# PV in an encoder layer's attention: the exponentials as stationary operand, the attention rows turned in the output projection

## What is computed

```python
def one_block(qblk):
    s = jnp.einsum('bqhd,bkhd->bhqk', qblk, k, preferred_element_type=jnp.float32) * scale
    p = jax.nn.softmax(s, axis=-1).astype(v.dtype)
    return jnp.einsum('bhqk,bkhd->bqhd', p, v)
...
att = _attention(q, k, v)
mix = jnp.concatenate([a, att], axis=-1) @ w_out[i]
h = h + gm[:, None, :] * mix
```

## Time and profile before

| | |
|---|---|
| runs of the kernel, us | 2167.23, 2167.49, 2172.06; median 2167.49 |
| profiled execution: span, us | 2165.6 |
| its own time beside the span | the profile gives none; the median lies 1.9 above the span |
| TensorE matmul busy | 2039.0 us, 94% |
| VectorE busy | 1208.9 us, 56% |
| ScalarE busy | 531.2 us, 25% |
| GpSimd busy | 296.2 us, 14% |
| attention, first row of maxima to first matmul of the output projection | 981.5 to 1336.4 us |

### The profile page before, as it was taken

One profiled execution on the slowest core, in us unless ns is written; L12 is line 12 of the kernel. 1 busy time (PEld: TensorE's weight loads), 2 busy tenths in 40 slices (PEclk: granted clock), 3 DMA queues, 4 the chain that ended last, 5 costly groups with the idle time before them and its releaser, 6 DMA issues.

```text
span 2165.6 us, 22126 instructions
## 1 busy us (share of the span) xinstructions
PE 2039.0 (94%) x8778; PEld 1615.0 (75%) x8778; DVE 1208.9 (56%) x1465; ACT 531.2 (25%) x690; POOL 296.2 (14%) x218
## 2 busy tenths in 40 slices
PE   3999999999999999977888788999999999999998
PEld 2788888888888878864545455878888888888886
DVE  4665545445454466677988887354444334443336
ACT  3411111111111144255555543141111111111102
POOL 1000000000000010027768833000000000000001
PEclk7999999999999999997999999999999999999999
DMA  7344221222220240000000013021111011111001
GB/s 301 117 136 136 98 88 49 80 75 97 87 85 23 98 150 25 1 0 1 0 0 0 0 39 136 5 74 59 59 59 39 20 58 58 58 58 39 20 30 78
DMA packets 76600, 137.32 MB, mean 63 GB/s; under 512 B 3308, under 2 KB 56659, under 8 KB 76274
## 3 DMA queue, kind: packets, MB, share of 16 engines
q1 hardware_dynamic: 76530, 136.35, 18.2%
HBM read 127.94 MB, written 8.39 MB: 63 GB/s over the span
## 4 chain that ended last, share of the span: by engine, by line
PE 76%; issue 9%; DVE 8%; POOL 4%; ACT 2%; DMA 1%; SPq 0%; POOLq 0%; ACTq 0%; DVEq 0%
PE ps L304 46%; PE ps L350 22%; PE ps L1741 4%; PE ps L1652 2%; DVE cv L917 1%; DVE negmax L705 1%; POOL rqk L846 1%; DVE grow L784 1%; POOL cv L908 1%; DVE ada_acc L461 1%; PE ps L414 1%; DVE att L792 1%; DVE qkT L839 1%; PE ps L491 1%; POOL wor L1002 0%
## 5 line engine op out<-in xcount | busy, mean ns | idle before, releaser
L304 PE MATMUL ps<-xh,W 128*128 128x512 f32 x3072 | 966.4, 393 | 6.7 <-DVE xl L434 5.0
L304 PEld LDWEIGHTS ps<-xh,W 128*128 128x128 f32 x3072 | 578.0, 188 | 130.8 <-issue 6.2
L304 PE MATMUL ps<-xl,W 128*128 128x512 f32 x1536 | 599.5, 390 | 0.0
L350 PE MATMUL ps<-WD,AT 128*128 128x512 f32 x1920 | 441.2, 391 | 0.0
L350 PEld LDWEIGHTS ps<-WD,AT 128*128 128x128 f32 x1920 | 360.5, 188 | 77.4 <-issue 2.9
L328 DVE TENSOR_TENSOR tmp<-ps,tmp 128x512 f32<-128x512 f32 x88 | 60.9, 692 | 555.7 <-ACT tmp L322 555.7
L304 PEld LDWEIGHTS ps<-xl,W 128*128 128x128 f32 x1536 | 289.1, 188 | 59.8 <-issue 1.7
L360 DVE TENSOR_TENSOR H<-ps,H 128x512 f32<-128x512 f32 x352 | 240.6, 690 | 151.4 <-PE ps L350 151.0
L322 ACT ACTIVATE tmp<-ps 128x512 f32<-128x512 f32 x88 | 52.6, 598 | 748.9 <-PE ps L304 746.3
L399 POOL TENSOR_SCALAR stat<-stat 128x1 f32<-128x1 f32 x32 | 8.7, 271 | 1604.1 <-ACT XS L368 825.8
L908 POOL TENSOR_TENSOR cv<-cv,prod 128x1024 f32<-128x1024 f32 x60 | 155.9, 2619 | 58.6 <-ACT prod L900 58.5
(11 more groups left out here) (192 smaller groups left out, 1752.3 us busy)
## 6 DMA issues: line engine op xcount, KB each, us to landing
ada_raw<-in_w_ada SPq DMA_DIRECT2D x56, 512.0 KB, 4.3
rawd<-in_ffn_wd SPq DMA_DIRECT2D x22, 1024.0 KB, 4.9
rawg<-in_ffn_wg SPq DMA_DIRECT2D x21, 1024.0 KB, 5.1
rawu<-in_ffn_wu SPq DMA_DIRECT2D x21, 1024.0 KB, 7.4
ada<-in_w_ada SPq DMA_DIRECT2D x8, 1024.0 KB, 14.1
H<-in_x SPq DMA_DIRECT2D x8, 512.0 KB, 6.6
h_saved_rows<-H SPq DMA_DIRECT2D x8, 512.0 KB, 3.2
wor<-in_w_out SPq DMA_DIRECT2D x8, 512.0 KB, 3.4
```

The costliest lines, as they stand in the source:

```text
L304: mm = e.matmul(ps[:, bank], W1[:, c, m, wx, kc], X[xx][:, kc, h * HALF:(h + 1) * HALF], start=(k == 0), stop=(k == 3 * KC - 1))
L350: mm = e.matmul(ps[:, 4 + k % DB], AT[:, par, c, ax, t * P:(t + 1) * P], wd[:, c, wx, h * HALF:(h + 1) * HALF], start=(n == 0), stop=(n == ...
```

## The change

PV changes operands. The exponentials of 128 keys by 128 queries become the weights, and `vs` streams through with 66 columns (64 values and 2 ones). A quarter p of a unit now works one tile of 128 queries over all 8 tiles of keys, in place of all 512 queries over two tiles of keys. The result has queries on partitions, four tiles of 66 columns in bank 6. ScalarE's copy is gone: VectorE takes four reciprocals per partition straight from PSUM and multiplies 4 x 64 values from PSUM into `att` (`dve_pv_out`), in quarter 0, after the quarter's maxima and its head split or tap. Bank 6 is then free (`pv_out`). Since `att` has queries on partitions, TensorE turns it tile by tile in the output projection (`pe_turn_att`, four 128x128 transposes for each of 8 token tiles, into banks 0 and 1), and `cut_mix` reads its part 1 from PSUM.

```diff
+        VA = VH + 2
...
-             ("vs", [P, 2, NT, 2 * VH], F32)],
+             ("vs", [P, 2, NT, VA], F32)],
...
                 if not (isinstance(i, int) and i == 0 and m == 1):
-                    e.wait_ge(pv_copied, i * 4 + (m - 1))
-            for kt in (2 * p, 2 * p + 1):
-                mm = e.matmul(ps[:, 6], vs[:, hp, kt], EX[(m - 1) % 2][:, kt], start=(kt == 0), stop=(kt == NT - 1))
+                    e.wait_ge(pv_out, i * 4 + (m - 1))
+            for kt in range(NT):
+                mm = e.matmul(ps[:, 6, p * VA:(p + 1) * VA], EX[(m - 1) % 2][:, kt, p * P:(p + 1) * P], vs[:, hp, kt],
+                              start=(kt == 0), stop=(kt == NT - 1))
...
-        def act_pv_copy(e, i, m):
...
-        def dve_pv_recip(e, i, m, third):
...
-        def dve_pv_scale(e, i, m):
+        def dve_pv_out(e, i, m):
...
+            got = ps[:, 6, 0:THALF * VA].rearrange("p (t d) -> p t d", t=THALF)
+            rec = grow[:, 0:THALF].unsqueeze(2)
+            e.wait_ge(pv_mm, i * 4 + m)
+            e.reciprocal(rec, got[:, :, VH:VH + 1]).then_inc(pv_rec, 1)
+            e.wait_ge(pv_rec, i * 4 + m)
+            dst = att[:, h * THALF:(h + 1) * THALF, bass.ds(chunk * 2 + hp, 1), :].rearrange("p t a d -> p t (a d)")
+            e.tensor_tensor(dst, got[:, :, 0:VH], rec.broadcast_to([P, THALF, VH]), ALU.mult).then_inc(pv_out, 1)
...
-                    if p == 0 and not (first and m < 2):
-                        act_pv_copy(e, *at(i, m - 1))
...
-                    if not (first and m < 2):
-                        if p < 3:
-                            dve_pv_recip(e, *at(i, m - 1), p)
-                        else:
-                            dve_pv_scale(e, *at(i, m - 1))
+                    if p == 0 and not (first and m < 2):
+                        dve_pv_out(e, *at(i, m - 1))
...
+            def pe_turn_att(t):
+                if t < 2:
+                    e.wait_ge(pv_out, NU * TURNS)
+                    e.wait_ge(ln_dve, 2 + CC)
+                else:
+                    e.wait_ge(mix_lo, cut_place(t - 2, 1))
+                for c in range(CC):
+                    mm = e.transpose(ps[:, t % 2, c * P:(c + 1) * P],
+                                     att[:, t, 2 * c:2 * c + 2].rearrange("p a d -> p (a d)"), ident[:])
+                mm.then_inc(att_turned, 1)
...
-            for m, part in ((0, 0), (1, 0), (0, 1), (1, 1)):
-                pe_mix(m, part)
-            for m in range(2, 2 * NT):
+            pe_mix(0, 0)
+            pe_mix(1, 0)
+            pe_turn_att(0)
+            pe_turn_att(1)
+            pe_mix(2, 0)
+            pe_mix(0, 1)
+            pe_mix(1, 1)
+            pe_mix(2, 1)
+            for m in range(3, 2 * NT):
+                if m % 2 == 1 and m // 2 + 1 < NT:
+                    pe_turn_att(m // 2 + 1)
                 pe_mix(m, 0)
                 pe_mix(m, 1)
```

More of the change, by code:

```diff
@@ L150, in build @@
             [("_g3", [P, KC, GW], F32), ("_u3", [P, KC, GW], F32), ("wkv", [P, 2, NHD * 2 * NOPE], F32R)],
-            [("slot", [P, 2, NT, QK], F32), ("qs", [P, NT, 2 * NHD], F32), ("_s2", [P, 384], F32), ("att", [P, CC, S], F32)],
+            [("slot", [P, 2, NT, QK], F32), ("qs", [P, NT, 2 * NHD], F32), ("_s2", [P, 384], F32), ("att", [P, NT, NHD, VH], F32)],
             [("wor", [P, 2, D], F32)])
@@ L237, in build @@
         s_mm, s_exp, pv_mm, pv_rec, pv_out = (sem(n) for n in ("s_mm", "s_exp", "pv_mm", "pv_rec", "pv_out"))
-        v_ok, pv_copied = sem("v_ok"), sem("pv_copied")
+        v_ok, att_turned = sem("v_ok"), sem("att_turned")
         ln_mean, ln_mm, ln_act, ln_pool, ln_dve = (sem(n) for n in ("ln_mean", "ln_mm", "ln_act", "ln_pool", "ln_dve"))
@@ L765, in pe_pv @@
                 if not (isinstance(i, int) and i == 0 and m == 1):
-                    e.wait_ge(pv_copied, i * 4 + (m - 1))
-            for kt in (2 * p, 2 * p + 1):
-                mm = e.matmul(ps[:, 6], vs[:, hp, kt], EX[(m - 1) % 2][:, kt], start=(kt == 0), stop=(kt == NT - 1))
+                    e.wait_ge(pv_out, i * 4 + (m - 1))
+            for kt in range(NT):
+                mm = e.matmul(ps[:, 6, p * VA:(p + 1) * VA], EX[(m - 1) % 2][:, kt, p * P:(p + 1) * P], vs[:, hp, kt],
+                              start=(kt == 0), stop=(kt == NT - 1))
             if p == THALF - 1:
                 mm.then_inc(pv_mm, 1)
-        def act_pv_copy(e, i, m):
[L774 to L777, removed]
-        def dve_pv_recip(e, i, m, third):
[L781 to L784, removed]
-        def dve_pv_scale(e, i, m):
+        def dve_pv_out(e, i, m):
             hp, h = (m - 1) % NU // NH, (m - 1) % NH
             chunk = i if m >= 1 else i - 1
-            e.wait_ge(pv_rec, i * 12 + 3 * m)
-            dst = att[hp * VH:(hp + 1) * VH, bass.ds(chunk, 1), h * HALF:(h + 1) * HALF].rearrange("p a q -> p (a q)")
-            e.tensor_tensor(dst, grow[0:VH, 0:HALF], grow[0:VH, HALF:D], ALU.mult).then_inc(pv_out, 1)
+            got = ps[:, 6, 0:THALF * VA].rearrange("p (t d) -> p t d", t=THALF)
[5 more added lines that the diff above has]
+            e.tensor_tensor(dst, got[:, :, 0:VH], rec.broadcast_to([P, THALF, VH]), ALU.mult).then_inc(pv_out, 1)
         def act_v(e, i, hp, first=False):
@@ L1030, in next_head, with cut_place @@
             return (i, 1) if m // NH == 0 else (i + 1, 0)
+        def cut_place(t, part):
+            return 2 * t + part + 1 if t >= 2 else 2 * part + t + 1
         def mix_src(part, t):
-            return (cv, att)[part][:, :, t * P:(t + 1) * P]
+            if part == 0:
+                return cv[:, :, t * P:(t + 1) * P]
+            return ps[:, t % 2].rearrange("p (c q) -> p c q", c=CC)
         MB = 3
@@ L1300, in _ @@
             run_units(e, unit)
-            act_pv_copy(e, TURNS, -1)
             act_ln_swish(e)
-            act_pv_copy(e, TURNS, 0)
             act_wo_hi(e, KC - 1)
@@ L1451, in _ @@
             e.wait_ge(U.mul, 8)
-            e.memset(vs[:, :, :, VH:2 * VH], 1.0).then_inc(k_ones, 1)
+            e.memset(vs[:, :, :, VH:VA], 1.0).then_inc(k_ones, 1)
             dve_tap0(e, 2, tap0)
@@ L1549, in cut_mix @@
                     e.wait_ge(s_mm, 4 * NU * TURNS)
-                if t == 0 and part == 1:
-                    e.wait_ge(pv_out, NU * TURNS)
+                if part == 1:
+                    e.wait_ge(att_turned, t + 1)
                 if t >= 2:
@@ L1555, in cut_mix @@
                 e.tensor_copy(dst, mix_src(part, t)).then_inc(mix_hi, 1)
-                e.wait_ge(mix_hi, 2 * t + part + 1)
+                e.wait_ge(mix_hi, cut_place(t, part))
                 dst = mixT[:, t % 2, LO, part * CC:(part + 1) * CC]
@@ L1559, in cut_mix @@
                                 ALU.subtract).then_inc(mix_lo, 1)
-            dve_pv_recip(e, TURNS, -1, 0)
-            dve_pv_recip(e, TURNS, -1, 1)
+            dve_pv_out(e, TURNS, -1)
             dve_ln_scale(e)
-            dve_pv_recip(e, TURNS, -1, 2)
-            dve_pv_scale(e, TURNS, -1)
             cut_mix(0, 0)
-            for third in range(3):
-                dve_pv_recip(e, TURNS, 0, third)
-            dve_pv_scale(e, TURNS, 0)
+            dve_pv_out(e, TURNS, 0)
+            cut_mix(1, 0)
             cut_mix(0, 1)
+            cut_mix(1, 1)
             dve_wo_lo(e, KC - 1)
             for t in range(NT):
-                if t + 1 < NT:
+                if 1 <= t < NT - 1:
                     cut_mix(t + 1, 0)
@@ L1733, in pe_mix @@
                     elif m == 2:
-                        e.wait_ge(pv_copied, NU * TURNS)
+                        e.wait_ge(pv_out, NU * TURNS)
                 if h == 0:
-                    e.wait_ge(mix_lo, 2 * t + 1 + part)
+                    e.wait_ge(mix_lo, cut_place(t, part))
                 for c in range(part * CC, (part + 1) * CC):
```

## The result

The changed kernel took 2262.43 us (median of 5 runs, 2234.21 to 2266.82) against 2167.75 us; the ratio is 1.0407, with a 95% interval of 1.0354 to 1.046. It is slower, as forecast, but by 94.7 us where the forecast of 2215.5 had 47.75: the median lies at the upper edge of the range, which went to 2262. The runs spread by 33 us, those of the kernel before by 5. The profiled execution was the quickest of the five (span 2232.4 us); a later one of the same kernel (run after_again) had a span of 2260.5.

The account below looks back on a forecast made before the run. TensorE bounds the kernel, sharing the bound with VectorE in the attention. Schedule +7, clock +38 and output projection +3 make +48 on the 2165.6 us span, 2213.6; the median lies 1.9 above, so 2215.5 us, range 2174 to 2262.

Parts of the forecast that it names:

- rival 2: Attention: the clock stays low once fallen, half the attention at the low level, 7 + 75 + 3, 2252.5 us; chance 0.14.
- the signs that the prediction named: PV records 0.11 us apart; 3 to 6 us waits before PV, almost none before maxima; clock about 0.85; transposes unwaited.
- The price of PV: TensorE in PV: 16 records a quarter, 0.11 us apart, bounded by weight loads; 1.78 us a quarter, same as before.
- rival 3: PV on TensorE: load and columns add up, 0.055 us more a record, 56 us in all, 2271.5 us; chance 0.03.
- The schedule at full clock, +7: Attention: PV waits for VectorE's multiplication; a pair of units takes 41.0 us against 40.1, +7 us over 8 pairs.
- The clock, +38: Attention: waits before PV make the clock fall; some 120 us low against 43, half of the 77 more lost, +38 us.
- the fall to last like the long one, 6.8 us: Attention: each of 16 waits before PV brings a clock fall of 6.8 us, 109 us in all.
- The last PV, 14 us in place of 7.8: Last PV of the attention: 64 records starting at the low clock stay there, 14 us in place of 7.8.
- The output projection, +3: Output projection: eight groups of four transposes add 3.5 to 4.8 us on TensorE, VectorE's cuts hidden; +3 us net.
- The faster rival: Attention, even unit from `m_lo` to `pv_out`: tap and split undisturbed by GpSimd, pair 36.3 us, 2140.5 us; chance 0.07.

Follow-up runs that it names:

- after_again: The changed kernel once more, with no further edit: 2263.53 us, ratio 1.0424 to the kernel before.
- cols128: The changed kernel with 128 columns instead of 66 streamed by each PV matmul: 2187.0 us, ratio 1.0069 to the kernel before.
- outfirst: The changed kernel, 66 columns, with VectorE's reciprocal and multiplication first in quarter 0, ahead of maxima and head split or tap: 2198.85 us, ratio 1.0123.
- both: The changed kernel with 128 columns and VectorE's reciprocal and multiplication first in quarter 0: 2150.1 us, ratio 0.99 to the kernel before.

## Why the prediction was right, and which terms were off

The direction, the place (attention), the output projection and the first half of the mechanism (a longer wait before PV, and a fall of the clock behind it) were right. The forecast had the clock come back after 6.8 us; that it does not is rival 2, which the prediction gave 0.14. The measured change is twice the forecast one. That the median still lies at the edge of the range (0.4 us past the rounded 2262) is owed to the upper end, which was laid just above rival 2, and not to the forecast's own working: that part is luck. Of the signs that the prediction named, the 0.11 us a record, the missing wait before the row and the transposes without a wait came; the mean clock over the attention was 0.72 and not about 0.85. Step by step:

- **The price of PV.** 0.11 us a record, 1024 records: held. A quarter runs in 1.9 us at full clock, its tail included (1.88 before). Load and columns do not add up even with 128 columns, where the columns alone take as long as the load: a quarter of 16 takes 1.95 us, its tail included. That is rival 3 gone. The rule behind it, of the Trainium skill's page "TensorE: Matmul & The Clock Gate", section "The mechanism", that loads overlap only matmuls of other row groups, is not borne out by these rows, in which each load fills all 128 rows.
- **The schedule at full clock, +7.** It can't be read from the changed kernel, which was at full clock for less than half of the attention: there TensorE's idle time fell by 14.6 us. The waits before PV were as worked out in the odd unit shown (3.21) but there were 13, 35.7 us in all, and not 16 of 3 to 6 (some 70); the waits before the row fell from 29.9 to 3.9 us. In a low spell VectorE is early, so fewer of its delays show (0.58 us before PV in the even unit of the spell above), and idle time and low clock could not be added as separate terms. cols128 has the same order at a clock of 0.87, and its idle time is 60.0 us, 1.7 more than before, so the term by itself was small, as said. One of its parts was too long: the even unit's wait before PV, 5.6 us by the prediction, is 3.25 in the even unit of cols128 shown above, where the head split took 2.2 us and not 4.0.
- **The clock, +38.** Right in kind, half in size. The step that failed is "the fall to last like the long one, 6.8 us". There were fewer falls than its 16, and they lasted longer: 12 spells of 19 us on the mean, four of them of 37.5 us and more. The low time came to some 230 us where it had 120. It also set out from too little: it took today's low time as 0.12 of the attention, 43 us, from the 0.94 of 1060 to 1300, and over the whole attention the kernel before has 0.91, some 65. TensorE's busy time in the attention rose by 76.7 us, and that is the term's measure. Rival 2 (low half of the time, 2252.5) had this size and this way: the low level took 55% of the attention in the profiled execution, and the median of 2262 is nearest to it. The sum is consistent: 76.7 - 14.6 + 3.4 = 65.5 for the profiled execution, whose span grew by 66.8.
- **The last PV, 14 us in place of 7.8.** Wrong. L976 (512 columns) ran at the low level, the clock rose 1.2 us into PV, and its 64 records took 7.84 us, at the high level to their end:

```profile
1388.29 3.72 PE L976 MATMUL ps<-pp,ones 128*128 128x512 f32 x4
1391.81 7.84 PE L770 MATMUL ps<-vs,E 128*128 128x66 f32 x64
```

```profile
1391.80:1395.50 3.70, 3.70 (x30) 3.69 (x28) 3.45 (x4) 2.19 (x2) 0.00 (x0) 0.84 0.00 0
1395.50:1399.40 3.90, 3.90 (x38) 3.90 (x36) 2.28 (x4) 2.44 (x3) 0.00 (x0) 1.00 0.00 0
```

- **The output projection, +3.** 3.4 measured, with the cuts hidden.
- **The faster rival** named the right place, the way from `m_lo` to `pv_out`, but as something that chance would shorten. Shortened by an edit, it is worth 64 us with 66 columns and 37 with 128, and together with the columns turns +4% into -1%.

## What to carry to other kernels

When operands are swapped so that each new set of weights serves few columns, price the load (here 0.11 us for 128 columns of float32 weights) and then ask what the half-empty stream does to the clock after the next wait; here, columns up to the length of the load cost no time of TensorE and paid by the clock. Put the instruction that frees a PSUM bank ahead of the work that nobody waits for (here the tap and the head split); before or behind the short maxima made no difference that these runs can tell. And do not add idle time and low clock as two terms: an engine that is slowed hides the delays of the others.

## What was not expected of the hardware

The same mix of PV with 66 columns and scores with 512 ran at either level with TensorE busy throughout: 15.8 us at 1.00 in one unit of outfirst, 28 us at 0.52 in another, 20 us at 0.50 in the changed kernel. Six spells of outfirst and four of the changed kernel ended after 27 to 55 us, and no change in what TensorE did stands out at their ends; what ends one is open. Redundant columns, 62 of 128, made the kernel 75 us faster. Some 12.6 us a unit (28.4 against 15.8) hang on the level at which it runs. The five runs of the changed kernel spread by 33 us, those of the kernel both by 11, with a mean clock of 0.93 over its attention.
